# The beginning of a fused block: eight buffers for the modulation weights, half of its sums as rows on TensorE, first products over half of the features

## The reference

```
mod = silu(c) @ w_ada + b_ada                 # c: one vector of 1024; six blocks of 1024 sums
sh1, sc1, g1, sh2, sc2, g2 = split(mod, 6)
h   = rms_norm(x, norm1_w) * (1 + sc1) + sh1  # x: 256 x 1024
p   = h @ w_in                                # q, k, v, z, a, beta, ...
qkv = silu(causal_conv(p[q, k, v]))           # 4 taps; then q and k are l2-normalised per head
o   = gated_delta_rule(q, k, v, g(a), beta)   # 8 heads, chunks of 64
```

## Time and profile before

| | |
|---|---|
| median of 3 runs | 920.41 us (917.84 to 920.51) |
| the profiled execution | 923.15 us, its span 921.3 us |
| PE, DVE, ACT busy, share of the span | 97%, 73%, 55% |
| first real product matmul | 39.65 us |
| mean DMA rate | 192 GB/s |
| 1 MB transfers of weights, issue to landing, medians by tensor | 4.7 to 5.7 us |

### The profile page before, as it was taken

How to read it: one execution, slowest core, us unless ns; L and a number is a source line. 1 busy time by engine, 2 the same in 40 slices (tenths; PEclk the granted TensorE clock), 3 DMA queues, 4 the chain that set the end, 5 groups by cost and what they waited for, 6 DMA issues and landing times.

```text
span 921.3 us, 18635 instructions
## 1 busy us (share of the span) xinstructions
PE 890.3 (97%) x8020; PEld 845.1 (92%) x8020; DVE 669.7 (73%) x1131; ACT 503.2 (55%) x811; POOL 68.1 (7%) x86
## 2 busy tenths in 40 slices
PE   6998999999999999999999999999999999999997
PEld 2798889999998899999999999999888999999997
DVE  3878876666979686668798785587656679888653
ACT  2489666444354646555364444466555566666442
POOL 0100201021011001020000001120000200000012
PEclk9999999999999999999999999999999999999999
DMA  8754323333767555465998889535322535555731
GB/s 334 267 187 176 120 111 126 105 138 132 253 232 255 196 216 195 172 211 175 274 336 308 278 280 252 211 103 219 138 105 80 184 132 201 217 184 172 251 127 46
DMA packets 27681, 177.31 MB, mean 192 GB/s; under 512 B 2864, under 2 KB 5680, under 8 KB 7504
## 3 DMA queue, kind: packets, MB, share of 16 engines
q1 hardware_dynamic: 27600, 176.13, 54.7%
HBM read 174.29 MB, written 1.84 MB: 191 GB/s over the span
## 4 chain that ended last, share of the span: by engine, by line
PE 83%; DVE 8%; ACT 6%; DMA 2%; issue 1%; SPq 0%; DVEq 0%; ACTq 0%
PE ps L1094 46%; PE ps L1100 22%; PE ps L1092 2%; DVE wl L1842 1%; ACT wh L1455 1%; PE ps L1139 1%; DVE acc L1741 1%; PE ps L1147 1%; PE ps L1233 1%; PE ps L1150 1%; PE ps L1098 1%; PE ps L1253 1%; DMA raw<-in_ada_dram 1%; PE ps L1207 1%; DVE KT L1724 1%
## 5 line engine op out<-in xcount | busy, mean ns | idle before, releaser
L1842 DVE TENSOR_TENSOR wl<-raw,wh 128x1024 fp32r<-128x1024 f32 x265 | 321.8, 1234 | 74.6 <-ACT wh L1455 74.0
L1094 PE MATMUL ps<-HH,wh 128*128 128x256 f32 x1480 | 371.9, 287 | 0.6 <-ACT HH L1429 0.2
L1094 PE MATMUL ps<-HH,wl 128*128 128x256 f32 x1480 | 358.6, 278 | 0.0
L1455 ACT ACTIVATE wh<-raw 128x1024 fp32r<-128x1024 f32 x265 | 273.5, 1042 | 150.8 <-PE ps L1100 118.5
L1094 PEld LDWEIGHTS ps<-HH,wh 128*128 128x128 f32 x1480 | 279.5, 189 | 9.3 <-issue 4.3
L1094 PEld LDWEIGHTS ps<-HH,wl 128*128 128x128 f32 x1480 | 279.2, 189 | 1.9 <-issue 1.9
L1100 PE MATMUL ps<-HL,wh 128*128 128x256 f32 x1480 | 227.2, 278 | 0.0
L1100 PEld LDWEIGHTS ps<-HL,wh 128*128 128x128 f32 x1480 | 195.8, 188 | 0.1
L1094 PE MATMUL ps<-FH,wh 128*128 128x256 f32 x352 | 84.5, 276 | 0.0
L1094 PE MATMUL ps<-FH,wl 128*128 128x256 f32 x352 | 84.5, 276 | 0.0
L1741 DVE SCALAR_TENSOR_TENSOR acc<-raw,silc,acc 128x512 f32<-128x512 f32 x101 | 76.3, 756 | 8.1 <-DMA raw<-in_ada_dram 5.0
(11 more groups left out here) (269 smaller groups left out, 1097.0 us busy)
## 6 DMA issues: line engine op xcount, KB each, us to landing
raw<-in_ada_dram SPq DMA_DIRECT2D x32, 1024.0 KB, 5.2
raw<-in_w_fi_dram SPq DMA_DIRECT2D x22, 1024.0 KB, 4.9
raw<-in_w_up_dram SPq DMA_DIRECT2D x22, 1024.0 KB, 4.8
raw<-in_w_rest_dram SPq DMA_DIRECT2D x20, 1024.0 KB, 4.8
raw<-in_w_in_dram SPq DMA_DIRECT2D x16, 1024.0 KB, 4.8
raw<-in_w_qkv_dram SPq DMA_DIRECT2D x12, 1024.0 KB, 4.8
raw<-in_w_o_dram SPq DMA_DIRECT2D x8, 1024.0 KB, 4.8
raw<-in_w_fo_dram SPq DMA_DIRECT2D x8, 1024.0 KB, 5.7
```

The source lines that it names most:

```text
L1094: e.matmul(o, w[:, k, 128 * t:128 * t + 128], x_hi[:, k0 + k, :], start=first and n + k == 0, **MM)
L1455: e.activation(whl[u % HALF][0][:, 0:n], raw[i % RAW][:, c:c + n], ACT.Copy).then_inc(*a_hi.up(u))
L1842: e.tensor_tensor(wl[:, 0:n], raw[i % RAW][:, c:c + n], wh[:, 0:n].bitcast(F32), ALU.subtract).then_inc(*v_lo.up(u))
```

## The change

It gives the eight early modulation transfers buffers of their own (in memory that the mixer's tensors use later), so that they and the first weights queue with no wait. Both halves of blocks 0 and 1 become rows on PE, blocks 2 and 3 stay sums on DVE. The products q0, k0 and v0 are fetched in halves and begin with feature blocks 0 to 3, in three banks at once; their second halves follow, then ab. The two groups of throw-away matmuls go. The clearing of G40 and `inv` moves behind the last `parts`.

```diff
-    for b, kp in ((2, 0), (0, 0), (2, 1), (0, 1), (3, 0), (1, 0), (3, 1), (1, 1)):
-        ada_item(b, kp, rows=b == 0 or (b, kp) == (1, 0))
-    for j in range(4):
-        product("q", j, a["w_in"][j], (HH, HL, N0))
-        if j == 0:
-            product("ab", 0, a["wab"], (HH, HL, N0), width=128, parts=((0, 1024),))
-        product("k", j, a["w_in"][4 + j], (HH, HL, N0))
-        product("v", j, a["w_in"][8 + j], (HH, HL, N0))
+    qkv = {"q": 0, "k": 4, "v": 8}
+    halved = [(open_product(kind, 0, (HH, HL, N0)), a["w_in"][qkv[kind]]) for kind in ("q", "k", "v")]
+    for n, (b, kp) in enumerate(((0, 0), (2, 0), (0, 1), (2, 1), (1, 0), (1, 1), (3, 0), (3, 1))):
+        ada_item(b, kp, rows=b < 2, early=n)
+        if n in (4, 6, 7):
+            piece(*halved[{4: 0, 6: 1, 7: 2}[n]], 0, 1024)
+    for p, w in halved:
+        piece(p, w, 1024, 1024)
+    product("ab", 0, a["wab"], (HH, HL, N0), width=128, parts=((0, 1024),))
+    for kind, j in [(kind, j) for j in range(1, 4) for kind in ("q", "k", "v")]:
+        product(kind, j, a["w_in"][qkv[kind] + j], (HH, HL, N0))
...
+    def first_half(n):
+        p = halved[n][0]
+        open_banks(p)
+        for t in range(2):
+            emit("mm", p["units"][0], t, None)
+
     def startup():
+        at = {it["ada"]: it["i"] for it in items if it["early"] is not None}
         emit("begin")
...
+        emit("ada_rows", at[0, 0], 5, None)
+        direct_norm(N0)
+        slot2 = acc.take()
+        emit("ada", at[2, 0], *slot2)
+        emit("ada_rows", at[0, 1], 5, None)
+        emit("ada", at[2, 1], *slot2)
+        row0 = turn(0, 5)
+        turned(0, row0)
+        reduce_now(2, slot2[0])
+        emit("ada_rows", at[1, 0], 6, None)
+        split_up_to(0)
+        emit("mod_scale", N0, 0)
+        for j in (0, 1):
+            scale(N0, j)
+        low_of(0)
+        for j in (0, 1):
+            parts(N0, j)
+        first_half(0)
+        emit("ada_rows", at[1, 1], 6, None)
+        slot3 = acc.take()
+        emit("ada", at[3, 0], *slot3)
+        split_up_to(1)
+        low_of(1)
+        first_half(1)
+        emit("ada", at[3, 1], *slot3)
+        row1 = turn(1, 6)
+        split_up_to(2)
+        low_of(2)
+        turned(1, row1)
+        reduce_now(3, slot3[0])
+        first_half(2)
+        split_up_to(3)
+        emit("mod_scale", N0, 1)
+        scale(N0, 2)
+        low_of(3)
+        scale(N0, 3)
+        for j in (2, 3):
+            parts(N0, j)
+        emit("zero")
+        for p, _ in halved:
+            run_unit(p, 1)
+            close_product(p)
...
-        if u == 0 and t == 0:
-            for _ in range(10):
-                e.matmul(o[:, 0:128], ones, eye, start=True, **MM)
...
-                if blk == 3:
-                    for _ in range(16):
-                        e.matmul(psum[b][:, 0:128], ones, eye, start=True, **MM)
```

More of the change, by code:

```diff
@@ L198, in _program @@
     d_raw = [signal(f"d_raw{i}", 16) for i in range(RAW)]
+    d_ada = [signal(f"d_ada{i}", 16) for i in range(EARLY_ADA)]
     d_dc, d_rb, d_u, d_out = (signal(n, 16) for n in ("d_dc", "d_rb", "d_u", "d_out"))
@@ L228, in _program @@
     sb("home_y", [128, 24])
+    early = ExitStack()
+    ada_buf = [sb(f"ada{i}", [128, 2048], where=early) for i in range(EARLY_ADA)]
+    early.close()
     mixer = ExitStack()
@@ L304, in _program, with item, buffer_of, landed @@
     cs = (c0, c1)
[L308 to L315, removed]
+    items, units, products, ring_items = [], [], [], []
+    def item(src, n, early=None, **kw):
+        it = dict(src=src, n=n, i=len(items), units=[], early=early, **kw)
+        if early is None:
+            turn = sum(x["early"] is None for x in items)
+            it["slot"], it["before"] = turn % RAW, ring_items[turn - RAW] if turn >= RAW else None
+            ring_items.append(it)
+        items.append(it)
+        return it
+    def buffer_of(it):
+        return ada_buf[it["early"]] if it["early"] is not None else raw[it["slot"]]
+    def landed(it):
+        return d_ada[it["early"]] if it["early"] is not None else d_raw[it["slot"]]
+    def ada_item(b, kp, rows=False, early=None):
+        item(a["ada"][b, :, 2048 * kp:2048 * (kp + 1)], 2048, ada=(b, kp), rows=rows, early=early)
     def unit(it, p, c, n, kn, width, k0):
@@ L321, in unit, with open_product, piece @@
         p["units"].append(u)
+    def open_product(kind, j, x, width=256, split=False):
+        p = dict(p=len(products), kind=kind, j=j, x=x, split=split, width=width, units=[], items=[], k=0)
+        products.append(p)
+        return p
+    def piece(p, src, at, n):
+        it = item(src[:, at:at + n], n, ada=None, rows=False)
+        p["items"].append(it["i"])
+        for c in range(0, n, 1024):
+            m = min(1024, n - c)
+            unit(it, p, c, m, m // p["width"], p["width"], p["k"])
+            p["k"] += m // p["width"]
     def product(kind, j, src, x, width=256, split=False, parts=((0, 2048),)):
[L324 to L327, removed]
+        p = open_product(kind, j, x, width, split)
         for at, n in parts:
[L329 to L334, removed]
+            piece(p, src, at, n)
     down = ((0, 2048), (2048, 2048), (4096, 1536))
     N0, N1, N2, N3, N4, N5 = range(6)
[L338 to L345 removed]
+    qkv = {"q": 0, "k": 4, "v": 8}
[9 more added lines that the diff above has]
+        product(kind, j, a["w_in"][qkv[kind] + j], (HH, HL, N0))
     for j in range(4):
@@ L427, in _program @@
     for it in items:
-        order += [("ada", it["i"])] if it["ada"] else [("u", u) for u in it["units"]]
+        if it["early"] is None:
+            order += [("ada", it["i"])] if it["ada"] else [("u", u) for u in it["units"]]
     def split_up_to(u):
@@ L470, in ada @@
             tasks.append(ada_reduce(b, sums[b][0]))
[L472 to L479, removed]
     def ada_reduce(b, slot):
         for _ in range(LATER):
-            yield
-        while b == 1 and ("turn", 1, 1) not in made:
             yield
@@ L495, in mod @@
     def mod(b):
-        until(*((("turn", n, 1) if n == 0 else ("red", n, 1)) for n in (2 * b, 2 * b + 1)))
+        until(("red", 2 * b, 1), ("red", 2 * b + 1, 1))
     part = []
@@ L915, in _program, with turn, turned, reduce_now @@
                 ("ug", 0): (high_first, ("uv", 0))}
+    def turn(b, bank):
+        slot, before = acc.take()
+        emit("turn", b, 0, slot, bank, before)
+        return slot
+    def turned(b, slot):
+        bank, before = misc.take()
+        emit("turn", b, 1, slot, bank, before)
+        acc.give(slot, p_misc, "turn", b)
+        misc.give(bank, v_misc, "mod", b)
+    def reduce_now(b, slot):
+        bank, before = misc.take()
+        emit("red", b, 0, slot, bank, before)
+        acc.give(slot, p_misc, "red", b)
+        emit("red", b, 1, slot, bank, reduced[-1] if reduced else None)
+        reduced.append(b)
+        misc.give(bank, v_misc, "red", b)
@@ L947, in _program @@
     startup()
-    for p in products:
+    for p in products[len(halved):]:
         if p["kind"] == "proj" and p["j"] == 0:
@@ L1022, in mod_ready, with raw_free @@
             v_misc.wait_ge(e, "mod", b)
-    def raw_free(e, i):
-        if i < RAW:
+    def raw_free(e, it):
+        if it["early"] is not None or it["before"] is None:
             return
-        it = items[i - RAW]
-        if not it["ada"]:
+        it = it["before"]
+        if it["ada"]:
+            v_misc.wait_ge(e, "ada", it["i"])
+        else:
             v_lo.wait_ge(e, it["units"][-1])
[L1030 to L1033, removed]
     def sync_engine(e):
@@ L1232, in tensor_engine @@
                     kt = 4 * kp + n
-                    ins = e.matmul(psum[b][0:1, :], silc[:, kt:kt + 1], raw[i % RAW][:, 512 * n:512 * n + 512],
+                    ins = e.matmul(psum[b][0:1, :], silc[:, kt:kt + 1], buffer_of(items[i])[:, 512 * n:512 * n + 512],
                                    start=kt == 0, **MM)
```

63 lines of the change are left out of this document (14 added, 49 removed).

## The result

The changed kernel took 932.88 us (median of 4 runs, 931.25 to 934.07), the kernel before 920.46 in runs beside it (917.84 to 922.1): 1.0129 of the time, with the interval 1.0087 to 1.0172. It is slower by 12.4 us, where I had forecast 921.8 us and a range that ended at 925.0. The profiled execution took 932.48 us, its span was 930.7, its mean granted clock 0.987.

What follows compares the result with a forecast made beforehand. ACT and DVE set the pace until about 96 us, PE after that; 0 for throw-away matmuls, -6.1 for the earlier start and +7.5 for waits gave +1.4 us on the median 920.41: 921.8 us, range 914.8 to 925.0.

Steps and rivals of the forecast that it cites:

- The start: Modulation and first units: transfers land in order, u5 ends at 49.85 us, PE 6.1 us ahead in work.
- my sum: Whole kernel: 0 for throw-away matmuls, -6.1 for PE's earlier start, +7.5 for new waits less old: +1.4 us; chance 0.52.
- Where the new wait is: q1's transfer waits for u4's `lo`, delaying q0's copy and convolution; PE idle from 49.85 to 52.9 us, at no cost.
- The order behind it: Convolutions, splits and decays on DVE and ACT after q0: `lo` of u11 ends at 70.55 us, against 70.6 before.
- The 3.1 us for `l2`: The first head's step 0 waits for `l2`: PE stands from 77.1 to 80.25 us.
- The waits that I listed: PE's new waits: 3.1 us for the bank, 1.5 for `lo` of u11 and u12, 3.1 for `l2`, 4.2 for table and `dec`.
- Rival C: Clock falls in the one gap where PE is then the bound: 3.1 us slower, 923.5 us; chance 0.18.
- the wait at 89.4: PE waits 4.2 us before the second head's step 1, for `dec`, table load and exponential.
- Where PE is then: Heads begin one unit earlier, moving PE work but taking none away; fourth `l2sum` ends at 101.7 us, against 100.3 before.

Runs made afterwards that it cites:

- run 2: Changed kernel with q1's splits moved behind the copies of q0 and k0: 926.20 us, 1.0061 of the kernel before.
- run 7: Changed kernel with q1's splits behind the copies of q0 and k0 and the heads' steps behind their old tiles: 921.92 us, 1.0015 of the kernel before.
- run 11: Changed kernel with only the heads' steps put back behind their old tiles: 923.32 us, 1.0011 of the kernel before.
- run 1: Changed kernel with 14 throw-away matmuls ahead of each of three PE waits: 929.52 us, 1.0099 of the kernel before.
- run 5: Kernel before with only its tick counter moved on by two, heads two tiles earlier: 925.47 us, 1.0050 of the kernel before.
- Run 10: Kernel before with only its tick counter moved on by one, first head behind tile 26 instead of 27: 927.55 us, 1.0066 of the kernel before.
- run 6: Kernel before with the modulation part of the change alone and the heads' steps in their old place: 919.56 us, 0.9975 of the kernel before.
- run 3: Kernel before with the modulation part alone, products whole in old order, throw-away matmuls kept, heads two tiles earlier: 924.28 us, 1.0029 of the kernel before.
- run 9: Modulation part alone, heads in their old place, plus 12 throw-away matmuls ahead of the first head's step 1: 921.10 us, 0.9985 of the kernel before.
- run 4: Kernel before without its 26 throw-away matmuls and nothing else: 918.89 us, 0.9978 of the kernel before.

## Why the prediction was wrong

**The start: right.** The first scale was forecast for 23.35 us and came at 23.30, the second for 38.2 and came at 39.06; transfers land one behind the other. The counts that I gave were wrong: by issue and landing at most eleven were outstanding (I had thirteen, all that are queued at the start less `vec`), and six before, four of them of 1 MB. u5 ended 1.5 us later than in my sum.

**Where the new wait is: right, a little small.** q1's transfer 45.57 for 44.1, landing near 50.4 for 48.9, the convolution 52.23 for 50.6. PE stood 3.3 us there, for 3.1 in my sum. Run 2 shows that this place in the queue is worth 6.7 us, though, as long as the heads stand early; with the heads in their old place it is 1.4 (run 7 against run 11), which can't be told from nothing. I had written that the wait costs nothing, since u7's bank and u8 wait on. With the heads early it does cost, by what hangs on q0's convolution further down DVE's queue: `lo` of u11 ended at 72.5, not at 70.55.

**The order behind it: a wait missed.** The second `l2sum` takes its bank from a ring of two, and the bank is held until ACT has copied V out. PE stood 3.4 us there (L1350 for V), and I had some 1.5 for the units around it. The 3.1 us for `l2` that I had at 77 us never came. The waits that I listed, 3.1, 1.5, 3.1 and 4.2, are 11.9 us, where my sum took 11.2 (7.5 and the 3.7 of before); measured from 45 to 110 us they are 9.9.

**The clock: three falls, not one.** Rival C had one, behind the wait at 89.4, at 1.7 us. All three gaps made it fall. The first two lie where PE waits again, as I had thought, and the third took 2.9. So the fourth `l2sum`, forecast for 101.7 us, ended at 109.1: 1.5 by u5, 2.0 less by the waits and 7.6 by the clock, of which my sum had nothing, make 7.1 of these 7.4. Keeping the clock up doesn't give the 7.6 back, since PE then waits instead: run 1 puts all of it at 3.4 us of the end time, with overlapping intervals. Rival C was right in kind and mis-sized by half: at that price it would have given 921.8 + 3.4 = 925.2. Its premise that the clock fell once before holds for the start and the heads; further on it fell twice more, near 680 and 704 us. And what stood ahead of the fall at the start was no single gap: eight matmuls of 1 x 1 run from 34.04 to 35.09 us, with 0.7 and 0.5 us idle around them.

**The step that failed** is in "Where PE is then": "the heads begin a unit earlier in the product stream, which moves work on PE but takes none away". It makes waits. A head's steps are short dependent pieces that PE, DVE, ACT and POOL hand to each other, set between tiles of products in queues that keep their order. Two tiles earlier, PE comes to the second head's step 1 before the `dec`, the table load and the exponential are done, and to later steps before `inv` and `y`. Runs 5 and 10 show it with nothing else changed (4.2 and 6.8 us), run 6 against run 3 on another kernel (4.7), run 7 against run 2 and run 11 against the changed kernel on that (4.3 and 9.6). Of the last three pairs only that of run 11 has intervals that lie apart, but all point one way. From the end of the fourth `l2sum` to that of the eighth, at the full clock, it is 56.8 us in the changed kernel and in run 5, and 54.0 and 54.2 in the kernel before and run 11. The wait ahead of the second head's step 1 had a place in my sum (4.2, measured 3.2), but the fall of the clock behind it and the waits behind 110 us had none.

So 11.0 of the 12.4 us are the heads' place and q1's splits ahead of q0's copy together; the last 1.4 is within what a measurement can tell (run 7 stands at [0.9988, 1.0041]). How the 11.0 divide depends on which is put back first: the heads 9.6 and then the splits 1.4, or the splits 6.7 and then the heads 4.3. The heads' place alone brings the changed kernel level with the one before ([0.9981, 1.0042]), the splits alone don't ([1.0030, 1.0091]). The third fall of the clock goes with the heads' place (no fall behind that wait in run 11); that run 1's 3.4 is part of the 9.6 is argued, not shown.

What stays open: for the 9.6 of run 11 the idle and lost time accounts for 5.9 and the first norm moves by 8.9; some 2 of the 3 us between are the faster rate from 360 us on, for which no run shows a cause, and how much of the 9.6 is due to it is not known. And the modulation with the heads in place (run 6) starts the products earlier and is still level with the kernel before. The chain says that what is gained at the start ends in the slack before 85 us. Run 9 was to show some of it: its first norm comes 2.2 us ahead of the kernel before, its time ([0.9947, 1.0023]) does not tell. No run beat the kernel before by more than can be measured; runs 4 and 6 come nearest, with intervals that end at 1.0004.

## What to carry to other kernels

Where a plan sets small dependent steps between large ones by a counter, an edit at the beginning moves all of them: compare the place of each step in each engine's order before and after, and hold it fixed while you measure the edit. When one engine's start moves forward by many microseconds, follow the rings and queues down to the first stretch in which it is the bound, and count there; what is gained before it is slack. Price a wait of 2 to 3 us on PE with the clock behind it, and only where PE is the bound.

## What the runs showed of the hardware that I had not expected

- At the same granted clock of 1.00 the stream of product matmuls goes at one of two rates: 179 in 20 us (before, 760 to 780 us) or 172 (run 9, the same stretch). The kernel before has both, 172 or 173 in some of the full stretches up to 440 us and 179 behind 740. Run 10's profiled execution, too, goes at 172 in 760 to 780 us. From the norm at 727.8 us to the last one run 9 took 191.0 us, the kernel before 184.0 from its norm at 729.9: 7 us with the clock at 1.00 throughout. Single runs of the kernel before lay between 915.8 and 932.2 us; this spread of rates may be the reason, which was not tested.
- The clock fell behind waits of 1.8 (run 2), 2.0 (run 4: 2.03 us for `qg`, then 0.50 in 88 to 90 us), 2.78 (run 6), 3.2, 3.3 and 3.4 us (after), and not behind one of 2.80. Near 320 us the same wait of 1.3 us has a fall behind it in run 4 (0.83 in 320 to 330 us) and none in the kernel before (1.00). The length of the wait alone does not decide, so the falls in one profiled execution may in part be chance.
- Eleven transfers outstanding on one queue did not share the engines: the first was used at 6.46 us, the second at 9.29, both as before (6.34 and 9.21).
